# Low parts of the fill weights: an accumulating DMA onto negated high parts in place of a subtraction on GpSimd

## The reference, cut to what matters

```python
def even_layer(x, mem, ...):
    h = rms_norm_2(x, norm_g) @ w_in
    gq, gk, gv, gb, ga, gg, dq, dk, dv, dg, mq, mg = split_cols(h, EV_SPLITS)
    y = jnp.concatenate([
        gdn_branch(gq, gk, gv, gb, ga, gg, ...),
        diff_attention(dq, dk, dv, dg, ...),
        memory_attention(mq, mg, mem, ...),
    ], axis=-1)
    return x + y @ w_out
```

## Time and profile before

| | |
|---|---|
| median of 3 runs | 2891.98 us (2890.57 to 2892.45) |
| the profiled execution | 2893.64 us, its span 2891.8 us |
| mean granted clock of TensorE | 0.955 |
| PE busy | 2561.8 us (89%) |
| DVE busy | 1440.4 us (50%) |
| ACT busy | 1109.0 us (38%) |
| POOL busy | 487.9 us (17%) |
| read from device memory | 520 MB, 182 GB/s over the span |

### The profile page before, as it was taken

One profiled execution on the slowest core, in us unless ns is written; L12 is line 12 of the kernel. 1 busy time (PEld: TensorE's weight loads), 2 busy tenths in 40 slices (PEclk: granted clock), 3 DMA queues, 4 the chain that ended last, 5 costly groups with the idle time before them and its releaser, 6 DMA issues. The chain is left out here.

```text
span 2891.8 us, 39412 instructions
## 1 busy us (share of the span) xinstructions
PE 2561.8 (89%) x14786; PEld 1893.3 (65%) x14786; DVE 1440.4 (50%) x2585; ACT 1109.0 (38%) x1975; POOL 487.9 (17%) x389
## 2 busy tenths in 40 slices
PE   8999999999888889999969979676899879958889
PEld 7984556885544444469858768565777657745667
DVE  5653883665211112247755544656455445454545
ACT  5544122453221222245444334343444334433434
POOL 0001010020111100000240220545300230052340
PEclk9999999999999999999979999788999989979999
DMA  7754334553699999935420145222344414421334
GB/s 297 224 201 150 142 135 153 181 199 119 275 422 422 422 422 421 384 138 176 163 80 18 45 160 189 73 102 73 131 147 180 168 69 160 153 99 41 132 116 146
DMA packets 80323, 529.79 MB, mean 183 GB/s; under 512 B 9089, under 2 KB 13569, under 8 KB 18849
## 3 DMA queue, kind: packets, MB, share of 16 engines
q1 hardware_dynamic: 76128, 514.50, 47.1%
q0 software_dynamic: 3456, 11.02, 1.5%
q10 hardware_dynamic: 576, 2.10, 0.2%
HBM read 520.24 MB, written 7.34 MB: 182 GB/s over the span
## 5 line engine op out<-in xcount | busy, mean ns | idle before, releaser
L753 POOL TENSOR_TENSOR ring_low<-ring,fill_wh 128x512 fp32r<-128x512 f32 x256 | 361.3, 1439 | 1159.7 <-ACT fill_wh L748 1159.2
L415 DVE TENSOR_TENSOR split_wl<-ring,split_wh 128x512 fp32r<-128x512 f32 x480 | 335.4, 706 | 251.5 <-ACT split_wh L383 250.0
L383 ACT ACTIVATE split_wh<-ring 128x512 fp32r<-128x512 f32 x480 | 300.7, 631 | 321.0 <-PE ps L355 317.4
L2296 PE MATMUL ps<-ring,yT 128*64 128x256 f32 x2048 | 247.9, 387 | 52.4 <-DMA ring<-in_weights 48.2
L353 PE MATMUL ps<-split_wh,x_high_part 128*128 128x512 f32 x672 | 267.9, 399 | 2.9 <-DVE split_wl L415 2.9
L354 PE MATMUL ps<-split_wl,x_high_part 128*128 128x512 f32 x672 | 266.1, 396 | 0.0
L355 PE MATMUL ps<-split_wh,x_low_part 128*128 128x512 f32 x672 | 266.0, 396 | 0.0
L786 PE MATMUL ps<-fill_wh,x_high_part 128*128 128x512 f32 x384 | 174.4, 454 | 77.8 <-PEq L2588 19.0
L2296 PEld LDWEIGHTS ps<-ring,yT 128*64 128x64 f32 x2048 | 137.8, 137 | 155.4 <-DMA ring<-in_weights 91.0
L1163 PE MATMUL ps<-ring,xT 128*128 128x512 f32 x512 | 222.0, 592 | 2.8 <-PEq L498 1.7
L748 ACT ACTIVATE fill_wh<-ring 128x512 fp32r<-128x512 f32 x256 | 145.3, 623 | 113.9 <-PE ps L788 51.6
(11 more groups left out here) (657 smaller groups left out, 5010.5 us busy)
## 6 DMA issues: line engine op xcount, KB each, us to landing
ring<-in_weights SPq DMA_DIRECT2D x468, 1024.0 KB, 5.3
x_res<-in_x SPq DMA_DIRECT2D x1, 2048.0 KB, 7.5
yT<-in_mem SPq DMA_DIRECT2D x1, 2048.0 KB, 15.5
rel_skew<-lru_feat POOLq DMA_DIRECT2D x1, 2048.0 KB, 50.0
mem_features<-yT ACTq DMA_DIRECT2D x4, 512.0 KB, 6.8
s_wb<-in_s_bc POOLq DMA_DIRECT2D x4, 512.0 KB, 4.1
s_wc<-in_s_bc POOLq DMA_DIRECT2D x4, 512.0 KB, 4.2
gate_bias<-in_gate_bias POOLq DMA_DIRECT2D x8, 256.0 KB, 4.0
```

Of the source, the lines that this page charges most:

```text
L383: nc.scalar.activation(wh[:, c % deep, :], raw(unit, turn, c), ACT.Copy).then_inc(w_high.sem, 1)
L415: last = nc.vector.tensor_tensor(wl[:, c % deep, :], raw(unit, turn, c), wh[:, c % deep, :], ALU.subtract)
L753: k.nc.gpsimd.tensor_tensor(self.low(step), k.ring[:, self.slot(step), self.columns(step)], self.high(step), ALU.subtract)\
L2296: last = nc.tensor.matmul(k.ps[s * WIN:(s + 1) * WIN, p, 0:FF], window[:, p, kc, :], k.ring[:, slot, at:at + FF], start=kc == 0, stop=kc = ...
```

## The change

1. ScalarE runs two activations per step in place of one: the high part as before, and then the same chunk times −1, rounded, written over the raw chunk in the ring slot. The signal `fill_high` comes after the second.
2. GpSimd no longer subtracts. It waits for `fill_high` and issues a DMA that reads the same 128x512 chunk (256 KB, 2 KB per partition) once more from device memory and adds it onto the negated high part, which leaves the low part. Eight semaphores, one per buffer, tell its landing.
3. TensorE waits for that semaphore of the step, in place of `fill_low`.
4. In `gemm_tokens` the first high parts of the fill come ahead of ScalarE's last eviction.

```diff
@@ -389,9 +389,9 @@
                             small.act(act)
 
                 each_block_late(act, blocks, upb, body)
-                finish((blocks - 1) // 2, (blocks - 1) % 2)
                 if fill:
                     fill.highs(act, 0)
+                finish((blocks - 1) // 2, (blocks - 1) % 2)
 
             @block.vector
             def _(dve):
@@ -745,13 +745,19 @@
         unit_wait(k, act, self.base + step // UNIT_KC, 0, 0)
         if n >= FILL_DEEP:
             act.wait_ge(used.sem, used.at(n - FILL_DEEP))
-        k.nc.scalar.activation(self.high(step), k.ring[:, self.slot(step), self.columns(step)], ACT.Copy).then_inc(high.sem, 1)
+        raw = k.ring[:, self.slot(step), self.columns(step)]
+        k.nc.scalar.activation(self.high(step), raw, ACT.Copy)
+        k.nc.scalar.activation(self.low(step), raw, ACT.Copy, scale=-1.0).then_inc(high.sem, 1)
 
     def make_low(self, pool, step):
-        k, high, low, n = self.k, self.k.ev("fill_high"), self.k.ev("fill_low"), self.number + step
+        k, high, n = self.k, self.k.ev("fill_high"), self.number + step
         pool.wait_ge(high.sem, high.at(n))
-        k.nc.gpsimd.tensor_tensor(self.low(step), k.ring[:, self.slot(step), self.columns(step)], self.high(step), ALU.subtract)\
-            .then_inc(low.sem, 1)
+        raw = k.dram["weights"][self.base + step // UNIT_KC][:, self.columns(step)]
+        pool.dma_start(self.low(step), raw, accum_op=ALU.add).then_inc(k.low_made[n % FILL_DEEP], 16)
+
+    def wait_low(self, pe, step):
+        n = self.number + step
+        pe.wait_ge(self.k.low_made[n % FILL_DEEP], 16 * (n // FILL_DEEP + 1))
 
     def highs(self, act, steps):
         upto = min(self.act_at + steps + FILL_LEAD, self.first[-1])
@@ -772,7 +778,7 @@
 
     def multiply(self, pe, steps):
         k, nc = self.k, self.k.nc
-        fill_a, fill_v, low, used = (k.ev(n) for n in ("fill_a", "fill_v", "fill_low", "fill_used"))
+        fill_a, fill_v, used = (k.ev(n) for n in ("fill_a", "fill_v", "fill_used"))
         for step in range(self.pe_at, min(self.pe_at + steps, self.first[-1])):
             n = max(m for m, at in enumerate(self.first[:-1]) if at <= step)
             (xh, xl), chunks, b, out = self.blocks[n]
@@ -780,7 +786,7 @@
             if kc == 0:
                 pe.wait_ge(fill_a.sem, fill_a.at(n - 1))
                 pe.wait_ge(fill_v.sem, fill_v.at(n - 1))
-            pe.wait_ge(low.sem, low.at(self.number + step))
+            self.wait_low(pe, step)
             for t in range(NT):
                 sums, at = k.ps[:, 6 + t, :], slice(t * P, (t + 1) * P)
                 nc.tensor.matmul(sums, xh[:, kc, at], self.high(step), start=kc == 0, stop=False)
@@ -4230,6 +4236,7 @@
         k.ps = ctx.enter_context(nc.psum_tensor("ps", [P, 8, BLK], F32))
         k.unit_loaded = [k.sem(f"unit_loaded{s}") for s in range(RING)]
         k.unit_used = k.sem("unit_used")
+        k.low_made = [k.sem(f"low_made{n}") for n in range(FILL_DEEP)]
         k.loaded = k.sem("loaded")
         k.first_loaded = k.sem("first_loaded")
         k.ones_made = k.sem("ones_made")
```

More of the change, by code:

```diff
@@ L178 @@
 EVENTS = ["evac_a", "evac_v", "x_high", "x_low", "w_high", "w_low", "w_used", "gated", "tr", "turn_ready", "ssq", "ms", "root", "scaled",
-          "fill_a", "fill_v", "fill_high", "fill_low", "fill_used", "small_mm", "mem_square", "mem_ms", "mem_root", "mem_scaled", "mem_turned", "mem_copied",
+          "fill_a", "fill_v", "fill_high", "fill_used", "small_mm", "mem_square", "mem_ms", "mem_root", "mem_scaled", "mem_turned", "mem_copied",
           "gather_high", "gather_low", "s_ask", "s_told", "decay_ask", "decay_told", "rel_made", "rel_copied", "gate_taken", "gate_biased",
```

## The result

The changed kernel takes 2980.65 us (median of 3, 2979.29 to 2987.76) where the kernel before takes 2891.98: a ratio of 1.0319 with a 95% interval of 1.0306 to 1.0333, 88.7 us more. The forecast was 2817, with a range of 2780 to 2905: the change was to gain 75 us and costs 89.

What follows compares the result with a forecast made beforehand. TensorE, busy 89% of the span, bounds the kernel; only its idle stretches caused by GpSimd can be gained. Gains of 101 us less 26 for ScalarE make −75 from 2893.6, as median 2817, range 2780 to 2905.

Steps and rivals of the forecast that it cites:

- part 1: Four GEMM ends: without subtractions and with high parts ahead of the last eviction, barriers fall 6.5 us sooner; 25 us gained.
- part 7: The accumulating DMA: low part 5.6 us after a step's first activation, against 8.2 of lead; latency and rate both hidden.
- Parts 2 and 3: Head norms and gdn input GEMM tail: VectorE no longer slowed by GpSimd's subtractions; 29 and 6.6 us gained.
- third rival: VectorE stays slow beside any work of GpSimd, descriptor writing included; gain only 25 us, 2867; chance 0.10.
- Part 4: Diff attention: TensorE's wait of 5.63 us per turn goes, less 1.3 a turn for late low parts; 20 us gained.
- Part 5: Smaller places: rope block 4 us, mla attention 5, two memory attentions 4 each, the rest 3.5; 20.5 gained.
- Part 6: ScalarE's second activation: 137 us of new work, a fifth of it on the path; 26 us lost.
- second rival: ScalarE becomes late: 60 of its 137 us fall on the path, gain 41 us, 2851; chance 0.14.
- first rival: Accumulating DMAs come slowly one behind another, mainly in diff attention; 65 us slower, 2957; chance 0.14.

Runs made afterwards that it cites:

- e1: The changed kernel with GpSimd's drain left out at the end of blocks that hold fill steps: 2822.83 us, 0.9767 of the kernel before.
- e10: e1 with a DMA that copies instead of adding, so the output isn't the reference's: 2791.76 us, 0.9667 of the kernel before.
- e11: e1 with one ScalarE activation per step, high part not made, so the output isn't the reference's: 2805.73 us, 0.9698 of the kernel before.
- e3: The changed kernel, drains kept, with the DMA copying instead of adding, so the output isn't the reference's: 2903.06 us, 1.0042 of the kernel before.

## Why the prediction was wrong, step by step

**The step that failed is the barrier in part 1, and the sentence on the DMA's low end in part 7.** Part 1 put the barrier at the end of ScalarE's eviction, "the barrier then falls at 1809.1 in place of 1815.64", and said that GpSimd's queue holds nothing else. It holds the block's drain, a term that the sum doesn't have. Part 7 weighed the landing against TensorE's need of a low part and found it hidden by 2.6 us; "at the low end the DMA costs nothing". TensorE's need was the wrong deadline. The real one is the end of the block, and there the landing is exposed whole. That is 126 us more of held barriers (175 against 49), and e1, which takes 165 of held time away, gives 158 back. The trace of before had a hint: the waits of the earlier trace rows are for barriers, and I read each as the length of the subtractions without asking which instruction of GpSimd the barrier waits for.

**The rest came out close, in part by luck.** Take e1, in which the drains no longer wait for landings: −68 us of −75 forecast, 2822.83 of 2817. But two costs are in it, 29 us of landings (e10) and 20 us of ScalarE (e11), where the forecast had 26 in all. So the gains, by estimate 68 + 49 = 117, were larger than the 101 forecast, and made up for the landings. Where the extra 16 come from isn't shown; one candidate is the clock, granted at 0.971 in e1 against 0.955, with TensorE busy for 2545.1 us against 2561.8.

- Part 1: VectorE starts 6.8 us sooner behind its eviction (its wait is 1.42 where it was 8.22), of 6.5 forecast; TensorE, which waits 2.52 us for the DMA, gains less.
- Parts 2 and 3: VectorE's slowing is gone wherever GpSimd only issues DMAs. Three lines of the changed kernel, from the answers for one line each, on the instructions of the earlier trace rows:

```profile
L3301 DVE SCALAR_TENSOR_TENSOR gdn_raw<-gdn_cv,cols_sb,gdn_raw x96: 472/478/485, 1307.0 to 1433.1; 128x256 f32<-128x256 f32 x96
```

```profile
L2938 DVE SCALAR_TENSOR_TENSOR att_scores<-att_scores,att_stat x16: 475/482/486, 1890.4 to 1979.5; 128x256 f32<-128x256 f32 x16
```

```profile
L2616 DVE TENSOR_TENSOR mla_in<-mla_in,head_stat x2: 1753/1756/1758, 2615.4 to 2617.1; 128x1536 f32<-128x1536 f32 x2
```

The maxima, 1512, 1612 and 2847 ns before, are now 485, 486 and 1758. The same holds for L2929, whose only large input is att_scores: 1450 ns at most before, 367 after. The third rival (VectorE stays slow beside any work of GpSimd) is refuted. The Trainium skill says in "SBUF — State Buffer", section "Who interferes with whom", that VectorE instructions with two inputs in SBUF contend with GpSimd's reads; these three lines agree with it. The trap that the same page of the Trainium skill describes in "SBUF: two separate sides", descriptor writing held up by VectorE, doesn't show: L756 takes 850 to 913 ns in the changed kernel. In e1 eleven of the 256 take over 950 ns, up to 2584, but most of these stand in one burst that began while VectorE was idle.

- Part 4, diff attention, was sized too large. From the first att_q to the last matmul the kernel before takes 130.1 us, e1 119.6 and the changed kernel 115.9, behind which its drain stands for 12 more: 10.5 gained in e1 of 20. With the copy (e10) it takes 112.5, which is 17.6 gained: so most of what is missing in e1 is the price of the addition. The DMA's rate had been taken as free at a share of 0.26. The stretch in the changed kernel, to the end of its drain:

```profile
core 0: us, PE busy (x) PEld busy (x) DVE busy (x) ACT busy (x) POOL busy (x), PEclk, DMA share, GB/s
1877.00:2004.90 127.90, 96.45 (x480) 75.76 (x480) 47.25 (x107) 78.92 (x180) 41.26 (x48) 0.93 0.85 198
```

VectorE needs 47 us where it took 74, but the DMA engines are now busy for 0.85 of it. The 1.59 us per addition lie above the 1.24 that the forecast had as its upper end. The halved rate of the Trainium skill ("Collectives: The Full Stack", section "The bandwidth ceiling: the fold count and why AG ≠ RS ≠ AR"), which had given an estimate of 1.06 us, points the right way, but the time is 1.59, and the ratio to e3's copy is 1.59/0.97 = 1.6 and not 2.

- Part 5: barrier to barrier, the two memory attentions gain 3.5 and 3.9 us in e1, of 4 each; mla attention gains nothing of the 5 (68.9 us against 68.3).
- Part 6: a fifth of ScalarE's new work on the path, 26 us; e11 shows 20. The second rival is refuted at its size of 60.
- Part 7, latency: 4.0 was taken for the landing, 7.3 measured (e1), and 0.86 for the issue in place of 0.56. The profile counts a landing from the start of its issue, so the forecast's sum had the issue in it twice. Without that it is 1.07 + 7.3 = 8.4 against 8.2 of lead. The 2.6 of slack wasn't there; this costs the 29 us of e10, of which a lead of seven buys 13 back.

**The first rival** had the right sign, and with 2957 the nearest time, but not the mechanism. It let the landings queue up inside diff attention, yet GpSimd issues as often as every 1.04 us with a landing of 8, so transfers overlap, and diff attention up to its last matmul is shorter than before. Its chance of 0.14 was for the wrong cause. For a mechanism that ends slower one should have asked of each new asynchronous operation which instruction waits for all of its kind.

## What to carry to other kernels

An operation that becomes asynchronous, that is, runs on after its issue, gets new deadlines: not only its consumer, but each drain and barrier behind its issue. Before an engine's work is handed to a DMA of the same engine, look for the drains at stage ends; where semaphores already guard the data, leave the drain out, and the same change may turn from a loss into a gain (here 1.032 to 0.977). And a lead in steps is to be measured against the landing of the very operation, and against what stands behind it in the queue of the engine that runs ahead.

## What the runs showed of the hardware that I had not expected

- GpSimd's drain ends with the landing of the DMAs issued on its queue: 8.83 us where the last landing took 8.5 (diff GEMM), 11.28 us with 10.9 (ahead of mla attention), and at 22 block ends of the changed kernel 0.12 to 2.0 us after the last landing. It doesn't wait for transfers that SyncE issued: the drain at 2133.42 took 0.05 us, while a ring load landed at 2135.6.
- A DMA that adds takes 7.2 us to land where one that copies the same 256 KB takes 4.2, 0.86 us to issue against 0.53, and 1.59 us of all 16 engines against 0.97.
- Ring loads of 1 MB landed in 7.1 us in place of 5.3 beside the additions, 6.0 beside the copies.
- VectorE is not slowed while GpSimd only issues DMAs (maxima of 485, 486 and 1758 ns, against 1512, 1612 and 2847 beside subtractions). All of this is float32 data; other types weren't tried.
